# Two transformer blocks on one core: values' tiles moved into the memory attention, and squares of five norms added up on GpSimd

## The reference

```python
for l in range(DEPTH):
    x = x + HALF_STEP * swiglu(rms_norm_2(x, ffn1_norm[l]), ffn1_w_gu[l], ffn1_w_down[l])
    x = x + hybrid_mixer(rms_norm_2(x, mix_norm[l]), positions, w_in[l], ...)
    x = x + memory_cross_attention(rms_norm_2(x, ca_norm[l]), rms_norm_2(mem, mem_norm[l]), ca_w_q[l], ca_w_kv[l], ca_w_o[l])
    x = x + HALF_STEP * swiglu(rms_norm_2(x, ffn2_norm[l]), ffn2_w_gu[l], ffn2_w_down[l])
return rms_norm_2(x, final_norm)

def rms_norm_2(x, g):
    y = x * rsqrt(mean(x * x, axis=-1) + NORM_EPS) * g

def swiglu(h, w_gu, w_down):
    g, u = split(h @ w_gu, 2)
    return (silu(g) * u) @ w_down

def memory_cross_attention(h, mem_n, w_q, w_kv, w_o):
    q = (h @ w_q).reshape(b, s, 4, 128)
    k, v = ...(mem_n @ w_kv)          # 256 memory tokens, 4 heads of 128
    p = softmax(q k^T / sqrt(128))
    return (p v).reshape(b, s, 512) @ w_o
```

## Time and profile before

| what | value |
|---|---|
| runs, median (lowest to highest) of 3 | 2827.11 us (2826.77 to 2829.59) |
| the profiled execution, its own time | 2828.48 us |
| its span | 2826.7 us |
| TensorE busy | 2671.7 us, 95% |
| VectorE busy | 1726.1 us, 61% |
| ScalarE busy | 1280.3 us, 45% |
| GpSimd busy | 152.8 us, 5% |
| mean DMA rate over the span | 140 GB/s |

### The profile page before, as it was taken

One profiled execution on the slowest core, in us unless ns is written; L12 is line 12 of the kernel. 1 busy time (PEld: TensorE's weight loads), 2 busy tenths in 40 slices (PEclk: granted clock), 3 DMA queues, 4 the chain that ended last, 5 costly groups with the idle time before them and its releaser, 6 DMA issues.

```text
span 2826.7 us, 45410 instructions
## 1 busy us (share of the span) xinstructions
PE 2671.7 (95%) x18697; PEld 2384.8 (84%) x18697; DVE 1726.1 (61%) x3239; ACT 1280.3 (45%) x2348; POOL 152.8 (5%) x174
## 2 busy tenths in 40 slices
PE   5999989999989989999999989899999999898998
PEld 4777567888868689999998879899999998698998
DVE  4554855454575566677545767666665557676763
ACT  3554644223255554454444445544544434454543
POOL 1000000000034410000000020000000000200000
PEclk9999999999989999999999999999999999899999
DMA  7555532232325334556554315366665553143653
GB/s 248 185 177 163 178 117 74 91 104 90 104 80 115 75 107 165 165 169 179 169 169 151 105 62 162 105 181 170 188 186 165 170 161 110 53 155 107 179 165 119
DMA packets 515678, 397.07 MB, mean 140 GB/s; under 512 B 26009, under 2 KB 491169, under 8 KB 515345
## 3 DMA queue, kind: packets, MB, share of 16 engines
q1 hardware_dynamic: 512672, 387.10, 45.1%
q0 software_dynamic: 2080, 3.53, 1.1%
q10 hardware_dynamic: 720, 3.54, 0.3%
HBM read 393.08 MB, written 1.05 MB: 139 GB/s over the span
## 4 chain that ended last, share of the span: by engine, by line
PE 85%; DVE 8%; ACT 3%; issue 1%; POOL 1%; DMA 1%; SPq 0%; DVEq 0%; ACTq 0%
PE pv L702 41%; PE pa L702 33%; PE pv L667 6%; PE pa L667 3%; DVE Wl L1745 2%; ACT Wh L1284 1%; PE pa L817 1%; PE pa L672 1%; DMA ring<-in_w_mod_dram 1%; POOL Pb L2344 1%; DVE Lb L1883 1%; DVE T L1804 0%; DVE T L1803 0%; DVE HTl L1752 0%; DVE TMP L1838 0%
## 5 line engine op out<-in xcount | busy, mean ns | idle before, releaser
L1745 DVE TENSOR_TENSOR Wl<-ring,Wh 128x1024 fp32r<-128x1024 f32 (+4 forms) x688 | 767.1, 1155 | 349.0 <-ACT Wh L1284 346.5
L1284 ACT ACTIVATE Wh<-ring 128x1024 fp32r<-128x1024 f32 (+4 forms) x688 | 647.9, 990 | 454.3 <-PE pv L702 451.3
L702 PE MATMUL pa<-HTl,Wh 128*128 128x256 f32 (+2 forms) x1648 | 537.7, 326 | 38.2 <-DVE HTl L1823 21.1
L702 PE MATMUL pv<-HTl,Wh 128*128 128x256 f32 (+1 forms) x1872 | 546.9, 292 | 15.3 <-DVE Wl L1745 5.0
L702 PE MATMUL pv<-HTh,Wl 128*128 128x256 f32 (+1 forms) x1872 | 537.9, 287 | 0.0
L702 PE MATMUL pv<-HTh,Wh 128*128 128x256 f32 (+1 forms) x1872 | 537.4, 287 | 0.0
L702 PE MATMUL pa<-HTh,Wl 128*128 128x256 f32 (+2 forms) x1648 | 523.6, 318 | 0.0
L702 PE MATMUL pa<-HTh,Wh 128*128 128x256 f32 (+2 forms) x1648 | 523.2, 317 | 0.0
L702 PEld LDWEIGHTS pa<-HTl,Wh 128*128 128x128 f32 (+1 forms) x1648 | 323.1, 196 | 73.6 <-issue 43.5
L702 PEld LDWEIGHTS pv<-HTl,Wh 128*128 128x128 f32 x1872 | 359.3, 192 | 29.5 <-issue 7.2
L702 PEld LDWEIGHTS pv<-HTh,Wl 128*128 128x128 f32 x1872 | 359.8, 192 | 3.0 <-issue 0.2
(11 more groups left out here) (231 smaller groups left out, 4025.0 us busy)
## 6 DMA issues: line engine op xcount, KB each, us to landing
ring<-in_ffn_w_gu_dram SPq DMA_DIRECT2D x176, 512.0 KB, 5.1
ring<-in_w_mlp_dram SPq DMA_DIRECT2D x64, 1024.0 KB, 5.3
ring<-in_w_in_dram SPq DMA_DIRECT2D x54, 1024.0 KB, 5.0
ring<-in_w_mod_dram SPq DMA_DIRECT2D x48, 1024.0 KB, 5.8
ring<-in_ffn_w_down_dram SPq DMA_DIRECT2D x64, 704.0 KB, 4.7
ring<-in_a_w_qkv_dram SPq DMA_DIRECT2D x12, 1024.0 KB, 5.3
ring<-in_b_w_qkv_dram SPq DMA_DIRECT2D x12, 1024.0 KB, 5.2
ring<-in_w_out_dram SPq DMA_DIRECT2D x8, 1024.0 KB, 5.2
```

Of the source, the lines that this page charges most:

```text
L702: m = nc.tensor.matmul(o, lhsT=x, rhs=y, start=first and j == 0, stop=last and j == 2)
L1284: ins = nc.scalar.activation(Wh[rows, p % SPLIT, a:b], ring[rows, i % RING, a:b], ACT.Copy)
L1745: ins = v.tensor_tensor(Wl[rows, p % SPLIT, a:b], ring[rows, i % RING, a:b], Wh[rows, p % SPLIT, a:b].bitcast(F32), ALU.subtract)
```

## The change

In the memory attention the weight blocks come in another order, and with them the work: queries 0 and 1 directly after keys 2 and 3; the two halves of the values behind the scores of units 1 and 2; queries 2 and 3 behind those of unit 3. VectorE's and ScalarE's copies and `prepare()` calls move with them.

For the norms of the four gated feed-forwards and for the last norm (`POOLED`), GpSimd adds squares 1 to 6 to square 0 in place, each addition waiting for its square and for the addition before it; TensorE multiplies only that sum and square 7 by the ones. The other norms stay as they are.

```diff
+NORMS = ([("n1", 0), ("n2", 0), ("n1", 1), ("n2", 1), ("nm",)]
+         + [key for l in range(DEPTH) for key in ((("f", l, 1), "n"), ("mix", l), ("ca", l), (("f", l, 2), "n"))] + [("fin",)])
+POOLED = [(("f", l, which), "n") for l in range(DEPTH) for which in (1, 2)] + [("fin",)]
...
-            by_columns(I["ca_w_kv_2"][l], 0, 2 * CA_W)
-            by_columns(I["ca_w_q_2"][l], 0, CA_W)
+            by_columns(I["ca_w_kv_2"][l], 0, CA_W)
+            columns(I["ca_w_q_2"][l], 0, 256)
+            by_columns(I["ca_w_kv_2"][l], CA_W, 2 * CA_W)
+            columns(I["ca_w_q_2"][l], 256, 256)
...
+                if key in POOLED:
+                    group(A, key, lambda b: b[:, 0:N],
+                          [(C("ones")[:, 0:P], squares(0)[:, 0:N],
+                            lambda: pe.wait_ge(sum_ready, seen.more(sum_ready, KT - 2))),
+                           (C("ones")[:, 0:P], squares(KT - 1)[:, 0:N],
+                            lambda: pe.wait_ge(sq_ready, seen.more(sq_ready, KT)))])
+                    return
...
-                for n in range(2):
-                    tokens_major(A, ("cv", l, n), split_slot(), [(MEM_AT, t) for t in range(2)])
                 linear(A, ("cq", l), 0, (0, P), hx, S, True)
                 pe.wait_ge(a_free, A.nth((("cq", l), 1)))
+                def scores(h, t, n, m):
+                    if (h, t) == (2, 0):
+                        pe.wait_ge(a_free, A.nth((("cq", l), 3)))
+                    return [(CQ[:, h, t * P:(t + 1) * P], CK[:, h, 0:n])]
+                def beside(i):
+                    if i < 2:
+                        tokens_major(A, ("cv", l, i), split_slot(), [(MEM_AT, t) for t in range(2)])
+                    if i == 2:
+                        linear(A, ("cq", l), 2, (0, P), hx, S)
+                def values(h, t):
+                    if t == 0:
+                        pe.wait_ge(a_free, A.nth((("cv", l, h // 2), 1)))
+                    return CV[:, t, h * P:(h + 1) * P]
...
+                def beside(i):
+                    if 1 <= i < 3:
+                        for t in range(2):
+                            copy((("cv", l, i - 1), t), CV[:, t, (i - 1) * 256:i * 256], lambda b: b[:, 0:256])
+                        prepare()
+                    if i == 3:
+                        queries((2, 3))
                 queries((0, 1))
-                attention(("mem", l), "mem", units("mem"), after=lambda i: queries((2, 3)) if i == 1 else None)
+                attention(("mem", l), "mem", units("mem"), beside)
...
-                for _ in range(4):
-                    prepare()
+                prepare()
...
-                          lambda i: prepare() if i == 1 else None)
+                          lambda i: prepare() if i < 4 else None)
...
+            def sum_squares(key):
+                at, a = NORMS.index(key) * KT, squares(0)[:, 0:S]
+                pool.wait_ge(sq_ready, at + 1)
+                for k in range(1, KT - 1):
+                    pool.wait_ge(sq_ready, at + k + 1)
+                    nc.gpsimd.tensor_tensor(a, a, squares(k)[:, 0:S], ALU.add).then_inc(sum_ready, 1)
+                    added[0] += 1
+                    pool.wait_ge(sum_ready, added[0])
...
             for l in range(DEPTH):
+                sum_squares((("f", l, 1), "n"))
...
+                sum_squares((("f", l, 2), "n"))
+            sum_squares(("fin",))
```

More of the change, by code:

```diff
@@ L433, in program @@
         sq_ready = sem("sq_ready")
+        sum_ready = sem("sum_ready")
         h_ready = sem("h_ready")
@@ L1214, in cross @@
                 linear(A, ("ck", l), 2, (0, P), mem, S)
-                for n in range(2):
-                    tokens_major(A, ("cv", l, n), split_slot(), [(MEM_AT, t) for t in range(2)])
                 linear(A, ("cq", l), 0, (0, P), hx, S, True)
                 pe.wait_ge(a_free, A.nth((("cq", l), 1)))
-                def last_queries(i):
-                    if i == 1:
-                        linear(A, ("cq", l), 2, (0, P), hx, S)
[L1223 to L1228, removed]
+                def scores(h, t, n, m):
[6 more added lines that the diff above has]
+                    if i == 2:
+                        linear(A, ("cq", l), 2, (0, P), hx, S)
+                def values(h, t):
+                    if t == 0:
+                        pe.wait_ge(a_free, A.nth((("cv", l, h // 2), 1)))
+                    return CV[:, t, h * P:(h + 1) * P]
+                attention(("mem", l), "mem", units("mem"), scores, values, P, lambda h: slice(0, P), behind=beside)
                 pe.wait_ge(v_free, V.nth((("mem", l), "O", len(units("mem")) - 1)))
@@ L1667, in cross @@
                         norm(("ca", l), LAT, RS, split=True)
-                for n in range(2):
-                    for t in range(2):
-                        copy((("cv", l, n), t), CV[:, t, n * 256:(n + 1) * 256], lambda b: b[:, 0:256])
-                    prepare()
                 def queries(js):
@@ L2322, in context_norm @@
                                         ALU.subtract).then_inc(cl_ready, 1)
+            added = [0]
+            def sum_squares(key):
[6 more added lines that the diff above has]
+                    pool.wait_ge(sum_ready, added[0])
             nc.gpsimd.memset(cT, 0.0).then_inc(c_zero, 1)
```

## The result

| what | before | after |
|---|---|---|
| median (lowest to highest) | 2827.11 us (2826.77 to 2829.59) | 2799.50 us (2799.03 to 2801.48), 4 runs |
| the profiled execution, its span | 2828.48, 2826.7 us | 2799.03, 2797.2 us |
| TensorE busy | 2671.7 us | 2645.3 us |
| GpSimd busy | 152.8 us | 180.1 us |

The account below looks back on a forecast made before the run. TensorE, 85% of the chain that ended last, was taken as the bound. Memory attention 12.0 us plus norms 6.3 us gave 18.3 us off, so 2808.8 us; own range 2805 to 2812.5, 8 in 10 from 2801.5 to 2815.5.

Parts of the forecast that it names:

- a sum over the touched places alone: Whole kernel: 12.0 us from both memory attentions plus 6.3 from five norms, 18.3 us off; other stages at nothing.
- 6.0 us a layer, bounds 4.9 and 6.8: Memory attention, each layer: time saved by the new order of work, 12.0 us for both layers.
- no wait for the latents: Memory attention: queries 0 and 1, moved ahead, find the normed latents ready, with 1.0 us of slack.
- the walk: Memory attention, layer 0: step-by-step timeline; scores 4 reach VectorE at 1801.8, output projection at 1812.1 with half-clock durations.
- Rival (b): Memory attention keeps its long TensorE wait; only 3.1 us a layer saved, 2814.5 us in all; chance 0.15.
- the 4.0 us: Memory attention: TensorE's idle wait of 4.02 us a layer in the kernel before, predicted to go.
- the 1.74 us: Memory attention: TensorE's wait for the second values' block to be split in the kernel before, predicted to go.
- put at 0.7 us: Second feed-forward of each layer: gain cut from 2.6 to 0.7 us because the second weight block is split late.
- a scaling waits for an addition: Feed-forward norms: VectorE's scaling is held by GpSimd's addition, 1.7 us a tile for 1.2; f-0-2's tile 7 slips 2.0.
- (a): Feed-forward norms: VectorE isn't held up by GpSimd's additions; 24.5 us off, 2802.6 us; chance 0.20.
- (c): Three feed-forwards: short waits ahead of the second weight block halve TensorE's clock; 14.1 us off, 2813.0 us; chance 0.10.
- (d): Norms: GpSimd's in-place additions far longer, slower from 2.0 us each; at 3 us each 2842.8 us; chance 0.03.

Follow-up runs that it names:

- delay 1: Kernel before with one more 0.43 us matmul of a square against ones in f-0-1's norm, product overwritten: 2820.62 us, ratio 0.9978.
- additions alone: Only the norms changed, but TensorE multiplies all eight squares after waiting for GpSimd's sum, so no matmul is saved: 2826.74 us, ratio 1.0011.
- queries first: Kernel before with queries 0 and 1 ahead of the values, all still ahead of the attention's first step, weight blocks in that order: 2827.52 us, ratio 1.0003.

## Why the prediction was wrong

The sign was right, the size was not: 9.3 us too little on the medians, 11.2 between the spans of the two traces (29.5 found for 18.3). The rows of the table by place account for the 11.2: 5.9 in the mixers, 2.5 in the attentions, 1.2 in the norms' places, and 1.6 ahead of f-0-1, which is of the size by which executions differ.

**The step that failed first: a sum over the touched places alone.** The prediction put every other stage at nothing, without a reason, and read half clock only where the diff lies. The runs showed 5.9 us there, 3.2 in mixer 0 and 2.7 in mixer 1. Mixer 0 has 19 to 20 us in which TensorE isn't busy (318.60 - 299.28), in many short waits, and whether the clock falls behind one depends on where it meets the clock's changes: 318.6 to 318.8 us when the first fall came 4.3 to 4.5 us after the norm, 315.3 to 315.5 when it came 3.9 to 4.1 us after, with 0.2 us between them. Further off it is neither (316.9 at 5.4, 317.6 at 2.6), and what happens at each short wait inside was not followed. The change put mixer 0 on the short side, because f-0-1 lost 0.35 us (delay 1 did the same with a matmul too many, and no pooled norm). Mixer 1 came out shorter with every kernel whose first fall there wasn't at 3.3 us. Which side a mixer falls on was luck: nothing in the change aims at it. The Trainium skill, "TensorE: Matmul & The Clock Gate", What's actually happening, says that the gate runs freely, not from the start of a kernel, so that the moment of a change of clock depends on where in it the matmuls fall; the runs agree that the place matters, with 315.3 to 323.5 us for the same mixer. They don't show it to be left to chance at a kernel's start: the two traced executions of the kernel before met the changes at the same place to 0.02 us. It was not weighed in the prediction, and it would have widened the range on both sides.

**The attention's "6.0 us a layer, bounds 4.9 and 6.8" was under-sized.** It measured 7.25, above the upper bound. The mechanism was right at each step: no wait for the latents, three groups of 48 at a clock of 1.00, the queries' and output blocks in turn, VectorE's pace at the end. Scores 4 came 44.75 us after the first keys (1796.96 - 1752.21) where the walk said 45.1, and from there to the output projection it took 8.26 us, the 8.3 that the prediction had worked out and then not used: it took a value between that floor and its walk at half clock, although its own reason (the idleness is gone) spoke for the floor. That is 0.8 us, and scores 4 came 0.4 us sooner than in the walk: 1.25 us a layer, 2.5 in all. Rival (b), that the 4.0 us stay, is excluded here. In "queries first" they do stay, with the 1.74 us as well.

**f-0-2 and f-1-2, put at 0.7 us, gave 1.8 each.** The step that failed is "a scaling waits for an addition". In these two the scaling slipped in by 0.07 us (but for the first addition's) and the low half waited instead, at every second tile: 0.6 us of slip where 2.0 were predicted, as in the kernel with the additions alone. In f-0-1, where the residual is taken by another line and the tiles come closer, five scalings of 0.89 to 0.91 us stood beside additions, as predicted, the block was 2.7 us late (2.4 predicted), and the norm gained nothing. f-1-1 gave its 2.6 us. The last norm gave 1.8 of its 2.1 us, and 0.25 were lost behind it.

**The rivals.** (a), no hold-up, would have been 2802.6, the nearest number, and is wrong all the same: VectorE is held, 0.55 us a meeting. (c) fell: the clock was 1.00 around and behind the waits for the second block in f-0-2 and f-1-2; in f-0-1 it fell among the tiles (0.80 from 1238.5 to 1246.9 us, where the kernel before had 1.00) and was 1.00 behind, and the chain there runs through VectorE, not TensorE. (d) fell: the additions took 0.92 us on average and 1.29 at most. The touched places' 21.9 us in place of 18.3, with nothing else, would have given 2805.2 us, inside the forecast's own range; the mixers' 5.9 took it out of both.

## What to carry to other kernels

A kernel whose TensorE has many short waits can have a time that depends on when each stage begins: before believing a gain or a loss of a few us, add one matmul ahead of the stage and see how much the time moves (here 0.43 us more gave 6.2 us less). Work that needs nothing from a latency-bound stage belongs between its steps; ahead of it, in either order tried here, it fills no wait inside it. When work goes to GpSimd, look at which operations of VectorE read two SBUF tiles beside it, and count meetings before GpSimd's time.

## What the runs showed of the hardware

- Mixer 0, with the same work on all engines, took between 315.3 and 323.5 us. TensorE spent 13.7 us of it at 1.2 GHz at 315.3 and 34.1 at 323.5 (mean clock 0.98 and 0.95).
- Two executions of one kernel whose spans differed by 2.1 us had both mixers equal to 0.02 us.
- Single runs of the unchanged kernel lay between 2819.6 and 2828.9 us in one set of 21, more than its first three runs suggested (2826.8 to 2829.6).
- An operation of VectorE on two SBUF tiles beside one of GpSimd ended 0.28 to 0.29 us after GpSimd's, whether another of GpSimd's followed at once or not; a held scaling (one SBUF tile) ended 0.15 us after it.
- Moving 17.3 us of squares' matmuls (five norms at 3.47 us) to two matmuls each cost GpSimd 27.6 us of additions, 30 of 0.92 us (0.73 the shortest; 0.92 to 1.29 where they began beside a weight split), and VectorE 7.1 us more busy time.
